# Halves of the small experts' tiles: transposed and summed on VectorE instead of folded on TensorE

## What is computed

```python
def moe_ffn(x, router_w, w1, w3, w2):
    logits = (xt @ router_w).astype(F32)                 # 256 tokens, 8 experts
    top_v, top_i = lax.top_k(logits, TOP_K)              # TOP_K = 2
    ...
    for e in range(N_EXPERTS):
        y = y + gates[:, e:e + 1].astype(x.dtype) * swiglu(xt, w1[e], w3[e], w2[e])

def swiglu(x, w1, w3, w2):                               # w1, w3: 1024 x 3584, w2: 3584 x 1024
    return (jax.nn.silu(x @ w1) * (x @ w3)) @ w2
```

## Time and profile before

| | |
|---|---|
| median of 3 runs | 2333.69 us (2332.4 to 2336.09) |
| the profiled execution | 2330.9 us, its span 2329.1 us |
| TensorE busy | 2288.7 us, 98% |
| VectorE busy | 1810.3 us, 78% |
| ScalarE busy | 1383.6 us, 59% |
| memory read | 580.07 MB, 250 GB/s over the span |

### The profile page before, as it was taken

The page is one execution under the profiler, slowest core; times in us unless marked ns, Lnnn a source line. Parts: engine busy times, 40 slices in busy tenths (PEclk is TensorE's granted clock), DMA queues, the critical chain, the costliest instruction groups (busy, mean ns, idle before and its releaser), DMA issues.

```text
span 2329.1 us, 29393 instructions
## 1 busy us (share of the span) xinstructions
PE 2288.7 (98%) x11211; PEld 1899.5 (82%) x11211; DVE 1810.3 (78%) x2342; ACT 1383.6 (59%) x1588; POOL 31.7 (1%) x44
## 2 busy tenths in 40 slices
PE   9999999999999999999999998999999999999998
PEld 7788887888888888787888877888888888888887
DVE  4865467989867687899899998899765569987655
ACT  4444444578755666788878874565544435654543
POOL 0000000000000000000000000000000000000000
PEclk9999999999999999999999999999999999999999
DMA  8366654699967799899999995644566565455663
GB/s 279 114 210 188 186 162 158 261 326 407 376 230 269 269 323 344 321 409 412 409 374 408 413 413 202 192 138 152 183 190 190 181 203 163 118 180 172 198 187 122
DMA packets 198508, 584.20 MB, mean 251 GB/s; under 512 B 17259, under 2 KB 26615, under 8 KB 183640
## 3 DMA queue, kind: packets, MB, share of 16 engines
q1 hardware_dynamic: 196060, 573.97, 70.1%
q0 software_dynamic: 1872, 6.82, 0.9%
q10 hardware_dynamic: 428, 1.45, 0.2%
HBM read 580.07 MB, written 2.12 MB: 250 GB/s over the span
## 4 chain that ended last, share of the span: by engine, by line
PE 88%; DVE 8%; ACT 1%; issue 1%; DMA 1%; DVEq 0%; POOL 0%; POOLq 0%; ACTq 0%; SPq 0%
PE tile L1005 19%; PE tile L1007 19%; PE tile L1006 19%; PE tile L1506 5%; PE tile L1507 5%; PE aux L1128 3%; DVE units_parts L2495 3%; PE aux L1492 2%; PE aux L1005 2%; PE aux L1006 2%; PE aux L1007 2%; PE aux L1507 1%; PE aux L1506 1%; PE aux L1419 1%; PE aux L1782 1%
## 5 line engine op out<-in xcount | busy, mean ns | idle before, releaser
L2495 DVE TENSOR_TENSOR units_parts<-units,high 128x1024 fp32r<-128x1024 f32 (+3 forms) x339 | 482.5, 1441 | 93.4 <-ACT high L1910 91.1
L1006 PE MATMUL tile<-units_parts,acts 128*128 128x512 f32 (+2 forms) x1344 | 515.0, 383 | 0.0
L1910 ACT ACTIVATE high<-units 128x1024 fp32r<-128x1024 f32 (+3 forms) x339 | 412.2, 1235 | 153.2 <-DMA units<-in_w_in 40.9
L1005 PE MATMUL tile<-high,acts 128*128 128x512 f32 (+2 forms) x1012 | 401.8, 397 | 6.5 <-DVE units_parts L2495 3.9
L1007 PE MATMUL tile<-high,acts 128*128 128x512 f32 (+2 forms) x1012 | 389.6, 385 | 0.0
L1006 PEld LDWEIGHTS tile<-units_parts,acts 128*128 128x128 f32 x1344 | 254.3, 189 | 47.1 <-issue 2.2
L1005 PEld LDWEIGHTS tile<-high,acts 128*128 128x128 f32 x1012 | 191.3, 189 | 44.9 <-DVE units_parts L2495 5.9
L1007 PEld LDWEIGHTS tile<-high,acts 128*128 128x128 f32 x1012 | 190.9, 189 | 38.5
L1006 PE MATMUL tile<-units_parts,zbuf_parts 128*128 128x512 f32 x328 | 127.6, 389 | 0.0
L1506 PE MATMUL tile<-high,params_parts 128*128 128x512 f32 x276 | 109.0, 395 | 0.0
L1507 PE MATMUL tile<-units_parts,params_parts 128*128 128x512 f32 x276 | 107.7, 390 | 0.0
(11 more groups left out here) (554 smaller groups left out, 5201.0 us busy)
## 6 DMA issues: line engine op xcount, KB each, us to landing
units<-in_moe_w SPq DMA_DIRECT2D x156, 1024.0 KB, 8.0
units<-in_w_in SPq DMA_DIRECT2D x134, 512.0 KB, 4.0
units<-in_w_ff SPq DMA_DIRECT2D x128, 512.0 KB, 3.7
q_buf<-in_moe_w SPq DMA_DIRECT2D x39, 1024.0 KB, 8.5
k_buf<-in_moe_w SPq DMA_DIRECT2D x39, 1024.0 KB, 8.2
nat<-in_moe_w SPq DMA_DIRECT2D x39, 1024.0 KB, 8.7
bias<-in_moe_w SPq DMA_DIRECT2D x39, 1024.0 KB, 9.0
units<-in_ffn_w SPq DMA_DIRECT2D x48, 512.0 KB, 3.7
```

Of the source, the lines that this page charges most:

```text
L1005: nc.tensor.matmul(bank, lhs[0], high, start=start, stop=False)
L1006: nc.tensor.matmul(bank, lhs[0], low, start=False, stop=False)
L1910: nc.scalar.activation(high_slot(SG[0], n) if wide_ else high_slot(SG[0], n)[:, 0:cols], halves(weights) if wide_ else weights[:, 0:cols], ...
L2495: V.tensor_tensor(low, weights, high, ALU.subtract).then_inc(SG[0].low_ready, 1)
```

## The change

A tile's raw result is now turned by `turn_raw`. The first matrix's four chunks are transposed whole (four 128 x 128 transposes into a bank of 512 columns) and VectorE adds the two halves with a `tensor_reduce`. In rounds 2 and 3 (`adds_both`) the second matrix's chunks are treated in the same way; in rounds 1, 5 and 7 they are folded as before. So a tile takes both spare banks where it took one. The SiLU works in place on the sum in SBUF, and in rounds 2 and 3 VectorE's product has both inputs in SBUF.

The places move too: tiles of a small expert are now taken one at a time, after units 9 and 10, 17 and 18, 25 and 26; those of round 2 after unit 4t + 6 where it was 4t + 5. The choice of rows and the gathers stand at other units, and the eight gathers that stood in step 8 for a round after 7 now stand at the start of that round, so they don't run here.

```diff
+def adds_up(r):
+    return few(r) or r == LARGE
+def adds_both(r):
+    return r in (LARGE, LARGE + 1)
+def added_after(r, i):
+    if r == LARGE:
+        return [i // 4 - 1] if i >= 6 and i % 4 == 2 else []
+    return [i // 4 - 2 + i % 8 - 1] if few(r) and i >= 9 and i % 8 in (1, 2) else []
...
 # TensorE
-                            bank = spare_bank("folded", r, t)
-                            for m in range(2):
-                                for c in range(4):
-                                    at = m * 4 * FEW + c * FEW
-                                    mm = nc.tensor.matmul(bank[:, at:at + FEW], raw_of(r, t, m)[:, c * P:(c + 1) * P],
+                        for m in range(2):
+                            bank = spare_bank("raw", r, t, m)
+                            for c in range(4):
+                                at = slice(c * P, (c + 1) * P)
+                                if m == 0 or adds_both(r):
+                                    mm = nc.tensor.transpose(bank[:, at], raw_of(r, t, m)[:, at], ident)
+                                else:
+                                    mm = nc.tensor.matmul(bank[:, c * FEW:(c + 1) * FEW], raw_of(r, t, m)[:, at],
                                                           fold[:, :], start=True, stop=True)
                             mm.then_inc(spare_full, 1)
...
-                            if k in BACK_GATHER and gathers(r):
-                                gather(r, BACK_GATHER.index(k))
...
 # ScalarE
+                    def silu_added(r, t):
+                        n = spare_at["raw", r, t, 0]
+                        act.wait_ge(spare_evac[n % 2], n // 2 + 1)
+                        nc.scalar.activation(product_of(r, t)[0], product_of(r, t)[0], ACT.Silu).then_inc(few_silu, 1)
...
 # VectorE
+            def add_halves(r, t):
+                banks = [spare_in("raw", r, t, m) for m in range(2)]
+                silu, linear = product_of(r, t)
+                for (bank, evacuated_), dst in list(zip(banks, product_of(r, t)))[0:2 if adds_both(r) else 1]:
+                    V.tensor_reduce(dst, bank[:, :].rearrange("p (c i n) -> p c n i", c=4, i=2), AX.X,
+                                    ALU.add).then_inc(evacuated_, 1)
+                if adds_both(r):
...
+                    dve.wait_ge(few_silu, C.folded.take() + 1)
+                    V.tensor_tensor(silu, silu, linear, ALU.mult).then_inc(few_added, 1)
+                else:
+                    bank, evacuated_ = banks[1]
+                    dve.wait_ge(few_silu, C.folded.take() + 1)
+                    V.tensor_tensor(silu, silu, bank[:, 0:4 * FEW].rearrange("p (c n) -> p c n", n=FEW),
                                     ALU.mult).then_inc(evacuated_, 1)
```

More of the change, by code:

```diff
@@ L236, in gathers @@
 def gathers(r):
-    return r <= LARGE or few(r) and r < ROUNDS - 1
+    return r <= LARGE or few(r) and r != N_EXP - 1
 def gathered_by(r):
-    return [r + 1, r + 2] if LARGE < r < N_EXP - 1 and gathers(r) else [r + 1] if gathers(r) else []
+    if not gathers(r):
+        return []
+    return [r] if r >= N_EXP else [r + 1] if r <= LARGE else [r + 1, r + 2]
 def few(r):
@@ L566, in product_of @@
             first = t % 2 * 4 if r == LARGE else 4 * t
-            return rows_.rearrange("p (c n) -> p c n", n=P)[:, first:first + 4, FEW:P]
+            both = rows_.rearrange("p (c n) -> p c n", n=P)[:, first:first + 4, :]
+            return both[:, :, FEW:P], both[:, :, 0:FEW]
         def hidden_few(r, t):
@@ L710, in build @@
         spare_evac = [sem(f"spare_evac{i}") for i in range(2)]
+        few_added = sem("few_added")
         raw_ready = sem("raw_ready")
@@ L1594, in first_matrices @@
                             if i == 0:
-                                for q in range(r):
+                                for q in range(r + 1):
                                     if r in gathered_by(q):
@@ L1603, in first_matrices @@
                                 turn_tile(back, LAST_TILE)
+                            if back is not None and i == tail_added_at(back):
+                                turn_raw(back, LAST_TILE)
                             if i in scatter_at(r) and late is not None:
@@ L1609, in first_matrices @@
                                 turn_tile(r, t)
-                            if i in GATHER_AT and gathers_within(r):
-                                gather(r, GATHER_AT.index(i))
+                            for t in added_after(r, i):
+                                turn_raw(r, t)
+                            if i in gather_at(r) and gathers_within(r):
+                                gather(r, gather_at(r).index(i))
                     def second_matrix(r, late):
@@ L1631, in expert @@
                         else:
+                            for k in range(8):
+                                gather(s - 1, k)
                             first_matrices(s - 1, None, s - 2)
@@ L2174, in first_matrices @@
                                 tile_in(back, LAST_TILE)
-                            if i == TAIL_AT + 2 and back is not None and (few(back) or back == LARGE):
+                            if back is not None and i == tail_added_at(back):
+                                silu_added(back, LAST_TILE)
+                            if i == tail_low_at(back):
                                 high_few(back, LAST_TILE)
@@ L2233, in expert @@
                             END[0] = C.unit.n + MOE_UNITS
+                            for k in range(8):
+                                gathered_in(s - 1, k)
                             first_matrices(s - 1, None, s - 2)
@@ L3112, in first_matrices @@
                         tile_in(back, LAST_TILE)
-                    if i == TAIL_AT + 2 and back is not None and (few(back) or back == LARGE):
+                    if back is not None and i == tail_added_at(back):
+                        add_halves(back, LAST_TILE)
+                    if i == tail_low_at(back):
                         low_few(back, LAST_TILE)
```

80 lines of the change are left out of this document (48 added, 32 removed).

## The result

The changed kernel takes **2351.65 us** (median of 4 runs, 2346.93 to 2355.91) where the one before takes 2333.43 (2332.4 to 2336.09): the ratio is 1.0078, its 95% interval 1.0059 to 1.0097. It is slower by 18 us. The profiled execution took 2351.8 us, its span 2350.0.

The account below looks back on a forecast made before the run. It took TensorE to bound steps 2 and 3, and VectorE to have no lead left between pairs in steps 1, 5 and 7. 9.0 + 9.4 + 8.6 - 13.2 = +13.8 us on 2333.69: 2348 us, range 2321 to 2362.

Parts of the forecast that it names:

- The handshake: Steps 1, 5, 7: SiLU waits for VectorE's sum, VectorE for ScalarE's split behind it; 3.14 us a tile, 11.8 a step.
- What idle time and lead absorb: Taken off VectorE's added time: 0.7 and 1.7 us in step 5, 0.4 more in step 1, 0.7, 3.2 and 2.0 in step 7.
- The seventh tile falls into step 6 and I take it as hidden: After step 5: the round's seventh tile costs nothing, hidden in VectorE's slack in step 6.
- TensorE's price: Four folds put off the next product by 0.87 us, four transposes by 0.40; each four replaced saves 0.47 us.
- Steps 2 and 3: TensorE is the bound there, so its 6.6 us saving in each comes through: -13.2 us, up to 4 at risk in step 3.
- the sums also hold up step 3 and step 2: Rival: TensorE waits there for VectorE to read the banks, taking back the 13.2 us: 2360, up to 2370 us; chance 0.11.
- The sums' price: Each of the 49 sums of 128 x 512 out of PSUM takes VectorE 0.69 us, bounds 0.49 and 1.0.
- TensorE is the bound everywhere: Rival, all changed steps: VectorE's additions hide and TensorE's saving shows, 20 us off: 2313 us; chance 0.21.
- Half price: Rival, steps 1, 5 and 7: the added wait costs 13.5 us instead of 27, so no change at 2334 us; chance 0.10.
- TensorE's own saving doesn't help: Steps 1, 5 and 7: TensorE's saving by transposes, 9.9 us in all, doesn't count because it then waits for VectorE.
- rival C: Rival named with the experiments, no chance given: the loss comes from the half-clock pieces that appear in the trace.

Follow-up runs that it names:

- the wait alone: Changed kernel with first matrices of rounds 1, 5 and 7 folded again; ScalarE's SiLU waits there for VectorE's copy of one column: 2338.63 us.
- the work alone: Changed kernel with first matrices of rounds 1, 5 and 7 folded again; VectorE does a sum-shaped tensor_reduce there that nobody waits for: 2318.65 us.
- folds and neither work nor wait: Changed kernel with first matrices of rounds 1, 5 and 7 folded again, SiLU reading TensorE's bank, no sum or wait for VectorE there: 2318.48 us.
- the later SiLU: Changed kernel with SiLU and product of rounds 1, 5 and 7 one unit after the sum: 2319.32 us; with rounds 2 and 3 too: 2313.65 us.

## Why the prediction was right

It said 2348 us with a range of 2321 to 2362, slower with a chance of 0.68; it is 2351.65. The mechanism was the forecast one. The terms were off by 2 to 6 us, and that the time still came out within 4 us is partly luck: what was charged too much to steps 1 and 5 made up for more than half of what was charged too little to step 7 and saved too much in steps 2 and 3.

**The handshake (steps 1, 5 and 7): right.** Predicted 3.14 us for a tile from the sum to the next low part, measured 2.99 and 2.98; for the wait with a copy 2.5, measured 2.46. Doing the wait alone, the work alone, both and neither shows it as the cause, and moving the SiLU takes it away. Of the signs that were named, TensorE's waits for low parts are there (26.6 us together, 4.2 before), but steps 1, 5 and 7 grew by 4.3, 4.7 and 8.9 us where 8 to 10 were expected of each.

**What idle time and lead absorb: mis-sized, in both directions.** Against the kernel with folds and neither work nor wait, the changed one spends 9.4 us more in steps 1 and 2 (1.7 of it a half-clock piece), 7.6 in 5 and 6, and 13.5 in 7 and 8. I had charged 11.8 to a step of a small expert and taken off 2.4 to 2.8. Against that control some 4 us vanish in each of steps 1 and 5. For step 5 part of the reason is a slip in my reading. Of the 4.7 us of idle time that I placed in the pairs, the 1.79 before 1156.92 lie behind the end of the stretch at 1155. What VectorE had outside the pairs was therefore not 1.0 us but 2.6, in four rows of the kernel before:

```profile
1101.65 2.29 DVE L2495 TENSOR_TENSOR units_parts<-units,gbuf_parts 128x2048 fp32r<-128x2048 f32 x1 [0.42 <-ACT gbuf_parts L1910]
...
1129.43 2.29 DVE L2495 TENSOR_TENSOR units_parts<-units,acts 128x2048 fp32r<-128x2048 f32 x1 [0.73 <-ACT acts L1910]
...
1133.26 2.29 DVE L2495 TENSOR_TENSOR units_parts<-units,gbuf_parts 128x2048 fp32r<-128x2048 f32 x1 [0.86 <-ACT gbuf_parts L1910]
...
1147.19 2.29 DVE L2495 TENSOR_TENSOR units_parts<-units,high 128x2048 fp32r<-128x2048 f32 x1 [0.62 <-ACT high L1910]
```

In the changed kernel 0.66 us are left of it at the same place in the list (0.44 and 0.22), so 2.0 were taken up where I had let 0.7 fall. With all 2.6 the term becomes 11.8 - 2.6 - 1.7 = 7.5, and steps 5 and 6 spent 7.6. That the rest of step 5, and step 1, follow in the same way fits but was not isolated. In steps 7 and 8 I had taken off 5.9 of 14.5 for a wait of 3.2 us on the weights, the lead at the last unit and idle time; of these only 1.0 shows, and more may be hidden under four half-clock pieces, 3.6 us by the one that could be priced (last section). The waits for weights did go, no such row is in the changed kernel's trace; how much time that gave back, the lengths don't show. Against before, the terms come to +7.3 (predicted 9.0) and +6.8 (9.4) in the run with rounds 1, 5 and 7 alone, and +11.0 (8.6) in the changed kernel.

"The seventh tile falls into step 6 and I take it as hidden" failed: step 6 grew by 1.7 us and, with rounds 1, 5 and 7 alone, step 2 by 2.5.

**TensorE's price: right.** Eight transposes in step 2 put off the next product by 0.79 us, as predicted:

```profile
682.34 1.03 PE L1548 MATMUL aux<-consts_sb,gbuf 128*128 128x128 f32 x8
683.13 0.48 PE L1054 MATMUL tile<-gbuf_parts,acts 128*128 128x512 f32 x1
```

A single record lasts 275 ns there on average, but the eight overlap:

```profile
L1548 PE MATMUL aux<-consts_sb,gbuf 128*128 128x128 f32 x192 | 27.1, 275 | 0.0
```

By the 275 ns that the Trainium skill (TensorE: Matmul & The Clock Gate, the part on the PE-mode transpose) gives for a transpose in a kernel, beside a figure for bf16, eight would have put it off by 2.2 us. The float32 record here agrees with that figure; as a price it is about three times too high where transposes follow one another.

**Steps 2 and 3: the size was off.** Predicted -13.2; the run with these rounds alone gave -7.1, or -8.8 without its half-clock piece. 2.14 us of the difference are the wait shown above, the handshake in a place that I had not looked at, the end of round 2. One tile of round 3 falls into step 4, which gave back 0.2 us. With the SiLU moved, steps 2, 3 and 4 together are 12.6 us shorter than before, nearly the whole, though 0.7 of it came with the change in round 1, whose seventh tile lies in step 2 (171.2 to 170.5 us). My rival "the sums also hold up step 3 and step 2" was thus partly true, at one place and for 2 us.

**The sums' price: right.** 686 ns for 0.69; the rows of VectorE in rounds 1, 3, 5 and 7 and the last tile of round 2:

```profile
L3142 DVE TENSOR_REDUCE zbuf<-aux 128x256 f32<-128x512 f32 x37 | 24.7, 686 | 2.4 <-PE aux L1550 1.6 <-PE aux L1548 0.7
```

The warning of the Trainium skill (VectorE: DVE Perf Modes, rules for kernel authors) against `tensor_reduce` on a hot path did not decide here: 21 of them cost 0.2 us by the medians where nobody waited.

**The rivals.** "TensorE is the bound everywhere" gave 2313 and needed a SiLU that doesn't wait for VectorE's place in its list. That is what the later SiLU does, and it takes 2313.65; for the kernel as it was changed the rival was wrong. The same number is partly chance, since it is made up otherwise: the rival let the DMA engines, at a share of 1.03, take all but 1 us of step 5's gain, and step 5 became 3.4 us shorter at the same share, while steps 7 and 8 gained nothing. "Half price" wanted 13.5 us for rounds 1, 5 and 7; alone they cost 28. "The sums also hold up step 3 and step 2" has a slip in its sum: 2360 and 15 us make 2375, not 2370; neither was reached. **"TensorE's own saving doesn't help"** in these rounds was right with the wait but for some 2 us (2349.63 with folds, 2349.01 with transposes). Without it, transposes make steps 1 and 5 shorter by 2.7 and 2.2 us than folds.

**Still open:** why steps 7 and 8 gain nothing from transposes with a later SiLU (145.8 us with one half-clock piece, 142.0 with folds and none). The seventh tile has no other step beside it there, which fits, but no run isolates it.

## What to carry to other kernels

Before moving work to an engine with idle time, look at what stands behind it in both lists. A step that took its input from TensorE and now takes it from VectorE ties two in-order engines together, and if each also feeds the other (split, low part), every such step costs a round trip, 2.46 us of VectorE's time here when its own work was a copy of one column. The remedy was not less work but one unit of distance: put the consumer behind the next piece that the other engine needs. High busy shares don't show this. What shows it is a producer whose busy share falls while its work grows, and two engines that name each other in the list of waits.

## What the runs showed of the hardware

**TensorE's granted clock falls to half for pieces of 3.4 us, and the piece costs 1.6 to 1.7 us where TensorE is the bound and almost nothing where it waits anyway.** With rounds 2 and 3 alone, TensorE's idle time of 2.12 us ended at 800.50, and the clock of the next stretch was 0.58, so at the lower level, 1.2 GHz, for most of it. First TensorE's row, then the two stretches:

```profile
800.50 0.47 PE L1584 MATMUL tile<-gbuf_parts,params_parts 128*128 128x512 f32 x1 [2.12 <-DVE gbuf L3206]
```

```profile
785.00:801.00 16.00, 13.88 (x65) 11.26 (x64) 10.88 (x10) 10.85 (x12) 0.00 (x0) 1.00 0.81 269
801.00:805.00 4.00, 4.00 (x12) 3.09 (x11) 4.00 (x4) 3.14 (x2) 0.00 (x0) 0.58 0.83 276
```

Step 3 took 132.8 us there and in the run with the wait alone, 132.9 in the second trace of the changed kernel, all with such a piece; it took 131.2 in the five traces of the same step without one. In those five TensorE waits at the same place, and no piece follows. In steps 1 and 5, where VectorE's chain sets the time, two pieces each in the run with rounds 1, 5 and 7 alone cost at most 0.5 us a step (110.8 and 115.5 us, against 110.3 and 115.1 without a piece). Steps 7 and 8 took 155.5 us with four pieces and 154.6 with three in the second trace of the same kernel, 0.9 for one. So rival C can claim about 1.7 us in step 2 and, if the other three cost what that one did, 4 x 0.9 = 3.6 in steps 7 and 8 (an estimate; at 1.7 each it would be 6.8), of the 30.5 that the changed kernel's steps 1, 2 and 5 to 8 take more than folds with neither work nor wait. The kernel before and that one have no piece in steps 1 to 8; what decides whether one follows a wait, these runs don't show.

**Steps repeat to a tenth of a microsecond between kernels.** Step 6 lasted 110.3 us in the kernel before and in four others in which no SiLU of rounds 5 to 7 waits for VectorE, while whole executions of one kernel differ by 8 to 14 us (2313.14 to 2321.17 with folds and neither, 2325.85 to 2340.09 for the kernel before). To find where a small edit acts, the length of a step from its semaphore tells more than the median.
